# A four-layer decoder on one core: the mixing product closed token tile by token tile, latent attention's output made per tile, the first FFN columns made for one tile alone

## What is computed

```python
for l in range(DEPTH):                       # DEPTH = 2
    h = rms_norm(x, pre_mix_g[l])
    z = h @ w_in[l]                          # split into the inputs of A, B, C, D
    o_a = hgrn2_mixer(...)                   # gated linear attention in chunks
    o_b = gla_mixer(...)                     # the same, another gate
    o_c = mla_mixer(...)                     # latent attention, causal softmax
    o_d = gdn_mixer(...)                     # gated delta rule in chunks of 64
    mix = jnp.concatenate([o_a, o_b, o_c, o_d], axis=-1).astype(h.dtype) @ w_out[l]
    x = x + rms_norm(mix, post_mix_g[l])
    h = rms_norm(x, pre_ffn_g[l])
    y = conv_glu_ffn(h, w_gate[l], w_up[l], ffn_conv_w[l], w_down[l])
    x = x + rms_norm(y, post_ffn_g[l])

def conv_glu_ffn(h, w_gate, w_up, conv_w, w_down):
    gate = causal_dwconv(h @ w_gate, conv_w)       # 2816 columns, 3 taps over the tokens
    return (jax.nn.gelu(gate, approximate=True) * (h @ w_up)) @ w_down
```

## Time and profile before

| | us |
|---|---|
| median of 3 runs | 1868.64 |
| range of the runs | 1866.43 to 1875.24 |
| the profiled execution's own time | 1874.93 |
| its span in the trace | 1873.2 |
| TensorE busy | 1716.1 (92%) |
| VectorE busy | 986.7 (53%) |
| ScalarE busy | 697.8 (37%) |
| granted TensorE clock, mean | 0.94 of full speed |

### The profile page before, as it was taken

The page is one execution under the profiler, slowest core; times in us unless marked ns, Lnnn a source line. Parts: engine busy times, 40 slices in busy tenths (PEclk is TensorE's granted clock), DMA queues, the critical chain, the costliest instruction groups (busy, mean ns, idle before and its releaser), DMA issues.

```text
span 1873.2 us, 28600 instructions
## 1 busy us (share of the span) xinstructions
PE 1716.1 (92%) x11756; PEld 1492.2 (80%) x11756; DVE 986.7 (53%) x1499; ACT 697.8 (37%) x1149; POOL 0.2 (0%) x4
## 2 busy tenths in 40 slices
PE   7999978999999998899999986899999997789998
PEld 7876568998887656899887765899888776689987
DVE  3244646775424464677724446566462444566545
ACT  2222434444222243544431125554351123455434
POOL 0000000000000000000000000000000000000000
PEclk9989998999998989899998987999998898799999
DMA  9300023555730001555553210455546401055653
GB/s 326 97 30 24 1 73 122 182 191 203 233 103 28 24 1 44 172 181 192 190 182 113 68 45 1 140 186 203 183 146 195 129 24 45 20 163 183 208 185 108
DMA packets 181954, 231.65 MB, mean 124 GB/s; under 512 B 12064, under 2 KB 161344, under 8 KB 181696
## 3 DMA queue, kind: packets, MB, share of 16 engines
...
## 4 chain that ended last, share of the span: by engine, by line
PE 85%; DVE 6%; ACT 4%; ACTq 1%; issue 1%; DVEq 1%; DMA 1%; SPq 0%
PE banks L412 84%; ACT all_work L2392 1%; DMA all_ring<-in_w_ple_gate 1%; ACTq L2396 1%; DVE all_ring_rounded L2535 0%; ACTq L2384 0%; ACT all_rest L2383 0%; DVE all_work L2611 0%; PE banks L2145 0%; DVE all_work L2587 0%; DVE all_rest L2696 0%; PE banks L888 0%; ACT all_ring_rounded L1303 0%; DVE all_mix_rounded L2543 0%; DVE all_ring_rounded L1546 0%
## 5 line engine op out<-in xcount | busy, mean ns | idle before, releaser
L412 PE MATMUL banks<-all_mix_rounded,all_ring_rounded 128*128 128x256 f32 x2432 | 448.6, 286 | 15.8 <-issue 10.3
L412 PE MATMUL banks<-all_ring_rounded,all_work_rounded 128*128 128x512 f32 (+1 forms) x1856 | 436.0, 372 | 12.1 <-DVEq L2734 6.9
L412 PE MATMUL banks<-all_work,all_ring 128*128 128x256 f32 (+5 forms) x2016 | 385.4, 358 | 31.9 <-DVE all_work L2557 8.8
L412 PEld LDWEIGHTS banks<-all_mix_rounded,all_ring_rounded 128*128 128x128 f32 x2432 | 386.3, 195 | 19.0 <-issue 10.6
L412 PEld LDWEIGHTS banks<-all_ring_rounded,all_work_rounded 128*128 128x128 f32 x1856 | 343.9, 191 | 72.1 <-DVEq L2734 7.6
L412 PEld LDWEIGHTS banks<-all_work,all_ring 128*128 128x128 f32 (+3 forms) x2016 | 325.4, 193 | 87.9 <-issue 34.7
L412 PE MATMUL banks<-all_work_rounded,all_ring_rounded 128*128 128x256 f32 x1216 | 347.4, 286 | 0.0
L2535 DVE TENSOR_TENSOR all_ring_rounded<-all_ring,all_ring_rounded 128x2048 fp32r<-128x2048 f32 x82 | 187.6, 2292 | 141.2 <-ACT all_ring_rounded L2379 140.0
L412 PEld LDWEIGHTS banks<-all_work_rounded,all_ring_rounded 128*128 128x128 f32 x1216 | 236.9, 195 | 0.0
L1546 DVE TENSOR_TENSOR all_ring_rounded<-all_ring,all_ring_rounded 128x2048 fp32r<-128x2048 f32 x74 | 169.4, 2292 | 86.6 <-ACT all_ring_rounded L1303 85.3
L2379 ACT ACTIVATE all_ring_rounded<-all_ring 128x2048 fp32r<-128x2048 f32 x82 | 156.3, 1908 | 108.2 <-DMA all_ring<-in_w_mlp_down 87.7
...
## 6 DMA issues: line engine op xcount, KB each, us to landing
...
```

Of the source, the lines that this page charges most:

```text
L412: ins = self.nc.tensor.matmul(out, lhsT, rhs, start=start, stop=stop)
```

## The change

**The mixing product.** The panels of `w_out` are regrouped: `out0` and `out1` hold row tiles 0, 1, 6, 7 (of the left and the right half of the columns), `out2` and `out3` row tiles 2 to 5. The first two are now loaded by two DMAs each. `early` makes row tiles 0, 1, 6, 7 of a bank (12 matmuls) and waits for A's and D's split alone; `rest` makes tiles 2 and 3 (6 matmuls) after B's; `late` makes tiles 4 and 5 of one token tile (12 matmuls in two banks) after C's split of that tile. The banks of token tile 0 are complete before `rest` and `late` of token tile 1.

**Latent attention.** The product with the values is made for token tile 0 as soon as its probabilities are turned (8 matmuls, bank `c_o0`), and for tile 1 later (16 matmuls, `c_o1`). VectorE splits each on its own (two instructions of 256 columns each instead of two of 512 for both).

**The order.** The "out" steps move from the stretch of B into that of A, so that panels are rounded and subtracted earlier. The list's end is now `... B15 C5 B16 B17 early1 mix2 C6 early2 C7 rest1 rest2 C8 C9 early3 early4 C10 late1 C11 rest3 rest4 late2`.

**The FFN's start.** TensorE transposes token tile 0 and makes gate columns j = 0 and 1 for its 128 tokens (48 matmuls); then it transposes tile 1, makes up columns j = 0 and 1 for tile 0 (48), and then gate and up of j = 0 and 1 for tile 1 (96). From j = 2 on all is as before. ScalarE's and VectorE's instructions for the two tiles are put in that order too: the work of tile 0 first, with the panels `gate0` and `up0`, then that of tile 1.

```diff
             view = self.t[:, n % SLOTS, 0:k * (c1 - c0)].rearrange("p (k n) -> p k n", k=k)
-            sp.dma_start(view, source).then_inc(self.full[n % SLOTS], 16)
+            for rows, columns, part in parts_of(source):
+                sp.dma_start(view[:, rows, columns], part).then_inc(self.full[n % SLOTS], 16)
...
+    def rows_of(half, n):
+        w = wout(512 * half, 512 * half + 512)
+        return w[:, 2:6, :] if n else [(slice(0, 2), ALL, w[:, 0:2, :]), (slice(2, 4), ALL, w[:, 6:8, :])]
+
+    late = [(f"1{layer}.out{2 * n + half}", rows_of(half, n), 4, 0, 512) for n in range(2) for half in range(2)]
     for i in range(FT // 2):
...
     HASTE = 0.94
     LEVEL_STEPS = len(LEVELS) + 3
-    GLA_STEPS, MLA_STEPS, GDN_STEPS = 3 + LEVEL_STEPS + 3, 10, 29
-    others = (interleave(["A"] * (GLA_STEPS - 2), ["in"] * 10) + ["A", "B", "A", "mix"]
-              + interleave(interleave(["B"] * (GLA_STEPS - 1), ["C"] * 4), ["out"] * 5))
-    ORDER = (["in"] * 10 + ["D"] + ["in"] * 7 + ["D", "in"] + interleave(["D"] * (GDN_STEPS - 2), others, HASTE)
-             + ["mix"] + interleave(["C"] * (MLA_STEPS - 4), ["early"] * 4) + ["mix"])
+    GLA_STEPS, MLA_STEPS, GDN_STEPS = 3 + LEVEL_STEPS + 3, 11, 29
+    A_side = interleave(["A"] * (GLA_STEPS - 2), ["in"] * 10)
+    for place in (23, 20, 17, 13):
+        A_side.insert(place, "out")
+    B_side = interleave(["B"] * (GLA_STEPS - 1), ["C"] * 5)
+    ORDER = (["in"] * 10 + ["D"] + ["in"] * 7 + ["D", "in"]
+             + interleave(["D"] * (GDN_STEPS - 2), A_side + ["A", "B", "A", "mix", "out"] + B_side, HASTE)
+             + ["early", "mix", "C", "early", "C", "rest", "rest", "C", "C", "early", "early", "C", "late", "C", "rest", "rest", "late"])
     made, squared = (turns_in(ORDER, {"A": LEVEL_STEPS + n, "B": LEVEL_STEPS + n, "D": GDN_STEPS - 6 + n}) for n in (3, 4))
 
 
     FIRST = 3
...
                         last = transpose(b[:, h * P:(h + 1) * P], Pr[t][:, h, kt * P:(kt + 1) * P])
                     last.then_inc(psum.full_of(f"c_pt{t}{kt}"), 1)
-            yield
-            pe.wait_ge(*due("PT", 3))
-            pe.wait_ge(*due("mla_v", 1))
-            b = psum.claim(pe, "c_o")
-            for h in range(4):
-                o, v = shaped(b, 4, P)[HD * (h % 2):HD * (h % 2) + HD], slice(HD * h, HD * h + HD)
-                mm(o[:, 2 * (h // 2)], vtokC[:, 0, v], PT[0, 0][:, h, :])
-                mm(o[:, 2 * (h // 2) + 1], vtokC[:, 0, v], PT[1, 0][:, h, :], True, False)
-                last = mm(o[:, 2 * (h // 2) + 1], vtokC[:, 1, v], PT[1, 1][:, h, :], False, True)
-            last.then_inc(psum.full_of("c_o"), 1)
-            yield
-            yield
+                yield
+                pe.wait_ge(*due("PT", 2 * t + 1))
+                pe.wait_ge(*due("mla_v", 1))
+                b = psum.claim(pe, f"c_o{t}")
+                for h in range(4):
+                    o, v = shaped(b[:, 0:T], 2, P)[HD * (h % 2):HD * (h % 2) + HD, h // 2], slice(HD * h, HD * h + HD)
+                    for kt in range(t + 1):
+                        last = mm(o, vtokC[:, kt, v], PT[t, kt][:, h, :], not kt, kt == t)
+                last.then_inc(psum.full_of(f"c_o{t}"), 1)
+                yield
 
...
             return last
 
         def mix_early():
             mixed.extend(psum.hold(4))
+            pe.wait_ge(*due("mix_split", 2))
+            for t in range(NT):
+                for half in range(2):
+                    psum.claim(pe, f"mix{half}{t}", mixed[2 * t + half])
+                    mix(t, half, PARTS["early"])
+                    yield
+
+        def mix_rest():
             pe.wait_ge(*due("mix_split", 3))
             for t in range(NT):
                 for half in range(2):
-                    psum.claim(pe, f"mix{half}{t}", mixed[2 * t + half])
-                    mix(t, half, (0, 1, 2, 3, 6, 7))
+                    mix(t, half, PARTS["rest"])
                     yield
 
-        emit(ORDER, {"in": project(), "A": gla(G["A"], 0), "B": gla(G["B"], 1), "C": mla(), "D": gdn(), "out": iter(range(5)), "mix": iter(range(3)),
-                     "early": mix_early()})
-        pe.wait_ge(*due("mix_split", 4))
-        for t in range(NT):
+        def mix_late():
+            for t in range(NT):
+                pe.wait_ge(*due("mix_split", 4 + t))
+                for half in range(2):
+                    mix(t, half, PARTS["late"]).then_inc(psum.full_of(f"mix{half}{t}"), 1)
+                yield
+
+        emit(ORDER, {"in": project(), "A": gla(G["A"], 0), "B": gla(G["B"], 1), "C": mla(), "D": gdn(), "out": iter(range(5)), "mix": iter(range(2)),
+                     "early": mix_early(), "rest": mix_rest(), "late": mix_late()})
+        psum.let_go(mixed[0:2])
+        kit.give_back(pe)
+        h = (rounded(mixT), rounded(hT))
+
+        def gate_up(j, half, tokens):
+
+            w = kit.split_panel(pe, ring, f"{('gate', 'up')[half]}{j // 2}")
+            c, b = (j % 2) * P, psum.bank(f"ff{j}")
+            for k in range(KT):
+                last = mm3(b[:, half * T + tokens.start:half * T + tokens.stop], [a[:, k, c:c + P] for a in w],
+                           [a[:, k, tokens] for a in h], k == 0, k == KT - 1)
+            if j % 2 and tokens.stop == T:
+                kit.free_panel(ring, f"{('gate', 'up')[half]}{j // 2}")
+            return last
+
+        kit.normed_transposes(pe, psum, "hT1", 2 * layer + 1, 0)
+        pe.wait_ge(kit.sems["h_split"], NT * layer + 1)
+        for half in range(2):
+            for j in range(AHEAD):
+                if not half:
+                    psum.claim(pe, f"ff{j}")
+                gate_up(j, half, slice(0, P))
+            if not half:
+                kit.normed_transposes(pe, psum, "hT1", 2 * layer + 1, 1)
+        psum.let_go(mixed[2:4])
+        pe.wait_ge(kit.sems["h_split"], NT * layer + 2)
+        for j in range(FT):
+            if j >= AHEAD:
+                psum.claim(pe, f"ff{j}")
             for half in range(2):
-                mix(t, half, (4, 5)).then_inc(psum.full_of(f"mix{half}{t}"), 1)
-        psum.let_go(mixed)
-        kit.give_back(pe)
-        for t in range(NT):
-            kit.normed_transposes(pe, psum, "hT1", 2 * layer + 1, t)
-        pe.wait_ge(kit.sems["h_split"], NT * (layer + 1))
-        h = (rounded(mixT), rounded(hT))
-        for j in range(FT):
-            b = psum.claim(pe, f"ff{j}")
-            for half, what in enumerate(("gate", "up")):
-                name = f"{what}{j // 2}"
-                w = kit.split_panel(pe, ring, name)
-                c = (j % 2) * P
-                for k in range(KT):
-                    last = mm3(b[:, half * T:(half + 1) * T], [a[:, k, c:c + P] for a in w], [a[:, k, :] for a in h],
-                               k == 0, k == KT - 1)
-                if j % 2 and not half:
-                    kit.free_panel(ring, name)
+                last = gate_up(j, half, slice(P, T) if j < AHEAD else slice(0, T))
             last.then_inc(psum.full_of(f"ff{j}"), 1)
-            if j % 2:
...
         names = [[f"mix{half}{t}" for half in range(2)] for t in range(NT)]
         kit.gained(dve, psum, 2 * layer, 0, names[0], gain_rows, yn)
         kit.added(dve, psum, 2 * layer, 0, names[0], yn)
         kit.scale_rows(dve, 2 * layer + 1, 0)
         subtract_rounded("gate0")
+        kit.lower_half_of_hT(dve, psum, "hT1", 0, PAR("pre_ffn"))
+        kit.split_h(dve, layer, 0)
+        subtract_rounded("up0")
         kit.gained(dve, psum, 2 * layer, 1, names[1], gain_rows, yn)
-        kit.lower_half_of_hT(dve, psum, "hT1", 0, PAR("pre_ffn"))
         kit.added(dve, psum, 2 * layer, 1, names[1], yn)
-        kit.split_h(dve, layer, 0)
         kit.scale_rows(dve, 2 * layer + 1, 1)
         kit.lower_half_of_hT(dve, psum, "hT1", 1, PAR("pre_ffn"))
         kit.split_h(dve, layer, 1)
-        subtract_rounded("up0")
         fw = shaped(PAR("ffn_conv"), FT, 3)
 
         def finish(j):
```

58 lines of the change are left out of this document (31 added, 27 removed).

## The result

The changed kernel takes 1877.24 us (median of 15 runs, 1873.64 to 1884.81); the kernel before, beside it, 1869.32 us (1866.43 to 1875.24). The ratio is 1.0039, with a 95% interval from 1.0027 to 1.0050: 7 us slower. The forecast was 8.5 us less, 1860. The time lies outside the range, and on the other side of the kernel before.

A forecast was written before the change was run, and what follows sets the result against it. TensorE, busy 92% of the span, was taken to bound the kernel. The three parts summed to -3.7 us in layer 0 and -4.8 in layer 1, so 1868.64 - 8.5 = 1860 us, range 1847 to 1871.

The forecast's parts named there:

- Part 1: Up to the first mixing matmul: three TensorE waits shortened, -4.6 us, against +3.3 for VectorE's queue and clock; -1.3 per layer.
- the 4.6 us: Ahead of mixing, per layer: waits saved at the last inversion level (0.6), B's head norm (1.4) and B's split (2.6).
- +3.3 per layer: Ahead of mixing: two waits behind subtractions added and one gone, 4.6 - 2.2 = 2.4 us, plus 0.9 for a slower clock.
- My worst end, +2.4 for the part: Stretch ahead of mixing, subtractions fully exposed: -3.2 + 4.6 + 1.0 = +2.4 us per layer.
- Part 2: Mixing: the slow clock at its head goes and 0.9 us of the wait for probabilities stays; -2.4 and -4.2 us.
- The -4.2 of the second layer: Mixing in layer 1: from 33.51 us down to 29.3, with 3.1 us of it gained from the clock.
- Part 3: End of mixing to second FFN column tile: narrow matmuls at 0.113 us fill idle time; 0.0 and +0.7 us, 33.1 in all.
- VectorE's queue eats the gain: Rival, ahead of mixing: subtractions fully exposed, +2.4 in place of -1.3 us per layer; 1867.5, no change; chance 0.14.
- Subtractions covered: Rival, ahead of mixing: A's output and `v_new` don't come late, -6.8 us, 5.5 better per layer; 1849; chance 0.14.
- Cheap narrow matmuls: Rival, FFN's start: matmuls of 128 columns take 0.081 us, 4.6 us less per layer; 1851; chance 0.10.
- The clock falls in the 128-column stretch: Rival, FFN's start: half the 144 matmuls at the lower clock, +8.1 us per layer; 1876, slower; chance 0.12.

The follow-up runs named there:

- experiment 2: The changed kernel with the rounding and subtraction of the panels of `w_out` put back in B's stretch, as before the change: 1892.47 us, ratio 1.0112.
- experiment 3: The changed kernel with 16 matmuls of constants added ahead of the wait for the squares of A's head-norm sum: 1873.98 us, ratio 1.0024.
- experiment 8: The kernel before the change with only the FFN's start in 128-column matmuls put in: 1883.50 us, ratio 1.0067.
- experiment 1: The changed kernel with the FFN's start undone on all three engines, as before the change: 1868.47 us, ratio 0.9998.
- experiments 5 and 6: The changed kernel with the old FFN start, plus A's head-norm sum one D-chain step later (5: 1862.02 us) or the last two "out" steps later (6: 1857.13 us).

## Why the prediction was wrong, point by point

**Part 1 is the step that failed.** Its gains were there: the wait behind B's split and that ahead of the last inversion level are gone, that behind B's head norm fell from 1.4 to 0.6. Of the 4.6 us 4.0 were gained. But the two subtractions, with the clock, were put at +3.3 per layer, and what came was 9.3 and 6.5: the stretch grew by 4.17 and 1.39 us with 1.15 less work in it, which makes 5.3 and 2.5, and 4.0 had gone on top of that. Split by what TensorE did in the stretch, the 9.3 are 3.4 of waits (its idle time fell by 0.6 only, with 4.0 gone) and 5.9 of low clock; the 6.5 are 3.4 and 3.2. Forecast were 2.4 of waits and 0.9 of clock. It failed in two ways.

*A place in the order was overlooked.* The change moved A's head-norm sum right behind the step that makes A's output. I read the two subtractions out of VectorE's list but priced them by the row in which one had cost 2.20 us, on a path with TensorE's work beside it. Here nothing stood beside it: the wait is 3.90, and experiment 2, with no subtraction there, still shows 2.9. The rows ahead of mixing had been compared, those around A's sum not.

*The clock was priced at 0.9 us.* This is the larger miss in both layers. The half speed lasts from the sum at 181.55 to about 205. Busy time grew by 4.8 and 2.0 us with 1.15 us less work, which makes 5.9 and 3.2 us; experiment 3 won back 2.6 and 2.3 of them. My worst end, +2.4 for the part, was too near: it put only 1.0 us on the clock.

**Part 2 was right** on the stretch: 29.3 us in both layers (29.2 and 29.3 forecast). The -4.2 of the second layer was read against an execution that was 1.8 us slow there (experiment 8). The clock at the head of mixing came back, since TensorE no longer idled ahead of it, and the wait for the probabilities is gone even further (0.7 for `c_o0` is left).

**Part 3 was right within 0.8 us.** 33.9 against 33.1, and 33.9 against 33.1 in the second layer too. The price of the narrow matmuls was right, the course of the stretch only in part. A matmul of 128 columns in the split form takes 0.113 us at full clock: the 144 run from 293.16 to 309.74, 0.115 each.

```profile
294.01 0.39 PE L421 MATMUL banks<-all_mix_rounded,all_ring_rounded 128*128 128x128 f32 x2
294.24 0.27 PE L421 MATMUL banks<-all_work_rounded,all_ring_rounded 128*128 128x128 f32 x1
294.35 0.39 PE L421 MATMUL banks<-all_mix_rounded,all_ring_rounded 128*128 128x128 f32 x2
```

These are three matmuls every 0.34 us. The first 48 took 0.175 on the mean, from 281.38 to 289.79, so that the idle 2.9 us ahead of tile 1's transposes were used up by the low clock and not saved: there is no wait ahead of those transposes. For the split ahead of the 48, put at 2.7 to 3.1, show 2.7 alone, and it took 2.73. The low clock took 3.0 us in the 48 and 1.4 in the transposes (3.4 in place of 1.95), 4.4 together, where I had put 0.6; that the sum still came near is luck, since 2.9 of it fell into idle time. What I missed is the comparison: I set the narrow start against the tail of before, not against the tail that the new mixing order gives without it, 30.1 (experiment 1). By that the narrow start was a loss of 3.8 us per layer.

**The rivals.** *VectorE's queue eats the gain* was the nearest, with the right place and too small a price: 1867.5 where 1877 was measured. *Subtractions covered* is refuted by the chain, on which both stand. *Cheap narrow matmuls*: refuted, 0.113; the 81 ns of the Trainium skill, "TensorE: Matmul & The Clock Gate", section "Back-to-back issue gap", are not met by matmuls in this float32 form (0.115 us over the 144). *The clock falls in the 128-column stretch*: it is low in its first part, in 8 down to 0.207 us per matmul, but it follows TensorE's waits ahead of it and rises again under the narrow matmuls themselves; the mean over the 144 is 0.115, below the 0.175 at which that rival decided.

**What stays open.** The stretches of the changed kernel account for 1.3 us, with the 1.15 us of work per layer that had moved ahead of them for 3.6, of the 7 us measured; with the 1.8 us by which mixing in the second layer was slow in the trace of before, some 5.4, an estimate. The rest lies within the scatter of the untouched code (10.7 us over the traces), and no run tells it apart. Open is also what makes the clock fall early in one layer and not in the other with the same instructions (experiments 5 and 6).
